# First layer's expert weights loaded with four consecutive rows per partition, context products on every fourth column

## The reference

```
def ec_moe(h, w_router, w_gate, w_up, w_down):
    cap = EC_FACTOR * T // N_EXPERTS
    aff = softmax(h @ w_router)
    gate, idx = top_k(swapaxes(aff, 1, 2), cap)     # each expert picks its tokens
    xe = h[idx]
    hid = silu(xe @ w_gate) * (xe @ w_up)           # per expert, 1024 x 1024 each
    ye = (hid @ w_down) * gate
    return zeros.at[idx].add(ye)
```

## Time and profile before

| | |
|---|---|
| median of three runs | 2534.03 us |
| the profiled execution, its own time | 2537.13 us |
| its span, first to last instruction | 2535.3 us |
| TensorE busy | 2368.9 us (93%) |
| loads by SyncE's and ScalarE's queues | 562.49 MB |

### The profile page before, as it was taken

The page is one execution under the profiler, slowest core; times in us unless marked ns, Lnnn a source line. Parts: engine busy times, 40 slices in busy tenths (PEclk is TensorE's granted clock), DMA queues, the critical chain, the costliest instruction groups (busy, mean ns, idle before and its releaser), DMA issues. The chain is left out here.

```text
span 2535.3 us, 36839 instructions
## 1 busy us (share of the span) xinstructions
PE 2368.9 (93%) x15152; PEld 1506.6 (59%) x15152; DVE 671.8 (26%) x1420; ACT 641.4 (25%) x1154; POOL 571.1 (23%) x320
## 2 busy tenths in 40 slices
PE   5999999999999799999999699999999789999888
PEld 3768878888887344444443477877888633333332
DVE  2271073211033211101111425064112432222223
ACT  4362263221233101111111535244223301100001
POOL 2142321344510001111111224333465000000000
PEclk9999999999998899999999799999999899999999
DMA  6271440221233699999999545343244599999996
GB/s 247 97 287 56 130 115 15 76 73 61 97 136 142 246 387 390 392 388 389 389 387 391 186 163 221 87 104 88 75 133 148 218 362 400 411 413 412 412 411 268
DMA packets 162383, 595.94 MB, mean 235 GB/s; under 512 B 16328, under 2 KB 57680, under 8 KB 143248
## 3 DMA queue, kind: packets, MB, share of 16 engines
q1 hardware_dynamic: 148368, 562.49, 58.7%
q0 software_dynamic: 10432, 25.99, 3.8%
q10 hardware_dynamic: 3488, 6.11, 0.8%
HBM read 576.63 MB, written 21.07 MB: 236 GB/s over the span
## 5 line engine op out<-in xcount | busy, mean ns | idle before, releaser
L473 PE MATMUL ps<-hi_r,ring_r 128*128 128x512 f32 (+1 forms) x1792 | 475.4, 354 | 3.9 <-POOL ring_r L2061 3.9
L1003 PE MATMUL ps<-ring_lo,zone 128*32 128x256 f32 (+1 forms) x3072 | 438.7, 493 | 23.2 <-DMA ring_lo<-in_w_gate 18.9
L473 PEld LDWEIGHTS ps<-hi_r,ring_r 128*128 128x128 f32 x1792 | 317.0, 190 | 51.5 <-POOL ring_r L2061 4.3
L1003 PEld LDWEIGHTS ps<-ring_lo,zone 128*32 128x32 f32 (+1 forms) x3072 | 156.3, 124 | 298.6 <-issue 271.2
L2061 POOL TENSOR_TENSOR ring_r<-ring_lo,ring_r 128x2048 fp32r<-128x2048 f32 (+1 forms) x58 | 240.1, 4144 | 364.9 <-ACT ring_r L1105 332.4
L473 PE MATMUL ps<-lo_r,ring_r 128*128 128x512 f32 (+1 forms) x896 | 315.7, 352 | 0.0
L1013 PE MATMUL ps<-zone 128*64 128x512 f32 (+1 forms) x2048 | 292.5, 496 | 2.3 <-issue 0.3
L467 PE MATMUL ps<-ring_r,hi_r 128*128 128x512 f32 (+1 forms) x736 | 227.7, 392 | 0.9 <-DVE lo_r L1600 0.9
L2170 POOL DMA_INDIRECT zone<-xn_dram,zone x36 | 40.5, 1125 | 812.1 <-DVE zone L2034 744.3
L1013 PEld LDWEIGHTS ps<-zone 128*64 128x64 f32 (+1 forms) x2048 | 111.5, 125 | 166.5 <-issue 146.1
L473 PEld LDWEIGHTS ps<-lo_r,ring_r 128*128 128x128 f32 x896 | 169.9, 190 | 23.3
(11 more groups left out here) (330 smaller groups left out, 2729.7 us busy)
## 6 DMA issues: line engine op xcount, KB each, us to landing
ring_lo<-in_w_gate SPq DMA_DIRECT2D x62, 2048.0 KB, 18.8
zone<-in_w_down SPq DMA_DIRECT2D x62, 2048.0 KB, 19.7
zone<-in_w_up SPq DMA_DIRECT2D x32, 2048.0 KB
ring_lo<-in_w_up SPq DMA_DIRECT2D x30, 2048.0 KB
ring_lo<-in_w_in SPq DMA_DIRECT2D x52, 1024.0 KB, 6.0
ring_lo<-in_ada_w SPq DMA_DIRECT2D x22, 2048.0 KB, 10.9
ring_lo<-in_w_branch SPq DMA_DIRECT2D x24, 512.0 KB, 6.3
zone<-v_dram SPq DMA_DIRECT2D x128, 64.0 KB, 1.9
```

The lines of the kernel that those rows point to most:

```text
L473: i = mm(dst[:, t0:t0 + tw], b[:, kk, f * P:(f + 1) * P], a[:, k, t0:t0 + tw], start=start and n == 0, stop=stop and n == 2)
L1003: i = mm(bank(((2, 4), (3, 5))[s // 2][gi])[j * M:(j + 1) * M, 0:W], xeT[:, k, c0:c0 + M], w[:, k % 4, j * W:(j + 1) * W], start=(k == 0), ...
```

## The change

`near_rows` is now true in both layers. What follows from it in the first layer:

- each unit is loaded with 16 KB runs (line 2302 in place of 2304, and the halves of lines 2291 and 2328 with 8 KB runs);
- the 8 transposes of the tokens and the 4 of the latent hidden values read their stationary operand with a step of four elements (16 bytes);
- GpSimd's queue makes the trip through `mod_dram` in the first layer too, and VectorE scales with `mxA` and `mxS`;
- the context groups of gate and up take columns j, j + 4, j + 8, ... of the weights in place of 256 neighbouring ones, so the moving operand of these products has a step of 16 bytes. Then the hidden value 4n + j stands in group j at column n, and the two context transposes of line 1060 stay contiguous; `out_half` takes `hidC` blocks in the new order.

The waits on `mod_out` count per layer, and the load of `iota` stays in the second layer alone.

```
         def near_rows(l):
-            return l > 0
+            return l >= 0
...
                             i = mm(bank(((2, 4), (3, 5))[s // 2][gi])[j * M:(j + 1) * M, 0:W], xeT[:, k, c0:c0 + M],
-                                   w[:, k % 4, j * W:(j + 1) * W], start=(k == 0), stop=(k == KD - 1))
+                                   w[:, k % 4, j::4] if gi else w[:, k % 4, j * W:(j + 1) * W], start=(k == 0), stop=(k == KD - 1))
...
-                                   hidL[:, k % 4, k // 4, :] if gi == 0 else hidC[:, k % 2, k // 2, :],
+                                   hidL[:, k % 4, k // 4, :] if gi == 0 else hidC[:, k // 4, k % 4, :],
...
                 if near_rows(l):
-                    dve.wait_ge(sem("mod_out"), 64)
+                    dve.wait_ge(sem("mod_out"), 64 * l + 64)
...
-                    pool.wait_ge(sem("mod_out"), 32)
+                    pool.wait_ge(sem("mod_out"), 64 * l + 32)
...
-                if near_rows(l):
+                if l > 0:
                     sp.dma_start(iota, A["iota"]).then_inc(sem("fills_in"), 16)
```

## The result

The changed kernel takes 2660.32 us (median of 4 runs, 2656.15 to 2661.08) against 2533.93 (4 runs, 2533.04 to 2534.76) of the kernel before on the same chip: 1.0492 of it, 95% interval 1.0479 to 1.0505, so 126 us slower. Its profiled execution took 2659.59 us with a span of 2657.7, 122.4 us over the span of before. The forecast was 2541, in a range of 2532 to 2560: the direction was right and the size was not.

The account below looks back on a forecast made before the run. TensorE was taken to bound the first layer's experts, loads the second's. Terms +8.0 + 0.3 + 1.0 - 1.1 - 1.0 = +7.2 us on 2534.0 gave about 2541 us, range 2532 to 2560.

Parts of the forecast that it names:

- What bounds the kernel: First layer's experts bound by TensorE, second layer's by loads; faster first-layer loads worth little, slower TensorE paid 16 times.
- Part 2, the moving operand: Context gate and up products with a step of four: 2 ns more per set over 512 sets, +1.0 us.
- A path that falls to half of its contiguous rate by the step would still give 1.13: Context products: half the merge products' 2.26 columns per ns nearly covers the 1.16 a set streams, supporting almost no cost.
- 33 ns per set: Rival for the context products: stream falls to the strided weight loads' rate, 13 to 33 ns more, 2552 us, chance 0.18.
- The rival of the four streams: Context products' four side-by-side streams get in each other's way: 2653 us two by two, 2880 one by one; chance 0.14.
- Part 1, the transposes: First layer's token and hidden-value transposes with a step of four: +0.50 us per expert, +8.0 us over 16.
- Nothing hides it: The transposes' longer weight load, 141 to 212 ns, is paid in full because TensorE is in order without idle time.
- The first gathered tokens: Their strided transposes ahead of the first layer's expert loop cost about one group's difference, +0.3 us.
- Part 3, the loads: First layer's loads land sooner and their queue stops growing: -1.1 us of waits and -1.0 us after the last expert.
- the last wait: TensorE's remaining waits for weights in the first layer's experts go away, -1.1 us.
- the handover: Chain from scatter to read-back after the first layer's last expert shortens: -1.0 us, bounds 0 and -4.
- Part 4, the trip: First layer's trip through `mod_dram` fits in GpSimd's wait for ScalarE: cost 0, about 17 us if uncovered.

Follow-up runs that it names:

- bench_streams: Kernel before plus fourteen blocks of products, one to four streams, contiguous or stepped, ahead of the expert loop; 256-column sets took 0.2175 us contiguous, 0.454 at step 4.
- stream_only: Kernel before with only the context gate and up products reading columns at a step of four; 2653.9 us, ratio 1.0462.
- no_stride: Changed kernel with the context gate and up products back on 256 neighbouring columns; 2534.41 us, ratio 0.9998.
- pairs: Changed kernel with context groups taking pairs of neighbouring columns, hidden values regrouped and context transposes at a step of two; 2540.88 us, ratio 1.0019.
- bench_types: Kernel before plus blocks of bfloat16 and float32r products and transposes at various steps; bfloat16 at steps 2, 4, 8 took 0.227, 0.451, 0.907 us.
- two_rows: Changed kernel with contiguous context columns, 8 KB runs for first-layer `w_down` and hidden transposes at a step of two; 2533.6 us, ratio 1.0.
- permuted: Changed kernel with the loads of two_rows, ScalarE and VectorE writing values in the order that makes all transposes contiguous; 2531.36 us, ratio 0.9995.

## Why the prediction was right or wrong

**What bounds the kernel** was read rightly, and it gave the direction: TensorE had no slack in the first layer's experts, so faster loads brought 2.5 us and slower products cost their full length.

**Part 2, the moving operand, failed:** taken at +1.0 us, measured at 16 x (41.28 - 33.51 - 0.16) = +122 us, with 33.51 for the pace of before without its waits and 0.16 for the transposes. Per set that is 0.238 us, and the benchmark has 0.454 - 0.2175 = 0.237. `stream_only` has it alone, 16 x 7.62 us, and `no_stride` takes it away. The step that failed is the sentence "A path that falls to half of its contiguous rate by the step would still give 1.13". It set the path's peak by the float32r products of the earlier trace rows and took "half" for the worst. But those products read four columns per line; if a change of line is what is paid, their own 0.227 us for 128 changes is already 1.77 ns each, and 256 changes make 0.454 us, the measured value. Four columns per line against one is a quarter of the rate, not half. (float32r itself does not follow this at a step of four, so that row fits the price but does not explain it.) The neighbour taken as nearest, the strided weight loads of the earlier trace rows, is another reader with another price: 0.118 us for 128 columns, 0.92 ns each, where the moving operand pays 1.77.

The Trainium skill (Advanced Engine Details and Errata, Memory Cachelines) has the rule that decided: at least two hits per 16-byte line, and a penalty for a different line each time. `pairs` and `bench_streams` agree with both halves, 0.226 us at two per line and 0.454 at one. It was cited and then given a price of its own only up to 33 ns per set.

**The rival of the four streams** had 2653 us, nearly the result, for the wrong reason: one stream alone is as slow as four. A time that fits does not show a mechanism.

**Part 1, the transposes, was over-sized:** +8.0 us forecast, 0.16 x 16 = +2.6 measured. The durations were right (1.10 us for the eight, 0.75 for the four, loads of 218 ns). "Nothing hides it" was wrong: the pause ahead of line 1013 fits a wait for ScalarE's copy that the profile doesn't name, and the longer transposes run into it. In the second layer the pause had been read as part of the price. The first gathered tokens cost nothing (1.52 us, before 1.51): TensorE has its lower clock there, where `bench_types` has 0.108 us contiguous and at most 0.120 with the step.

**Part 3, the loads, was right:** the last wait is gone, the landing is a steady 10 us in place of a growing one, and the handover gave 1.0 us, as taken. At TensorE's old pace (`no_stride`) the first layer moves 397 GB/s, the wait stays away and the handover is 1410.15 - 1388.55 = 21.60 us, so the form of the loads is enough for it. In the changed kernel it was not needed: `stream_only`, with the loads of before and the slower TensorE, has no such wait either, a steady landing of 11 us and a handover of 21.53. The number was right, but the changed kernel doesn't show which of the two brought it.

**Part 4, the trip, was right:** no cost, inside GpSimd's wait for ScalarE. TensorE's first gathered tokens come at 843.50 us, before at 842.65, but at 841.94 in `two_rows`, which makes the trip too.

The terms as measured, +122 + 2.6 - 1.5 (waits) - 1.0 = +122.1, make the 122.4 us between the two spans. That the two agree so closely is in part luck: the experts begin 0.85 us later than before, and the rest of the program behind line 514, 1125.2 and 1125.3 us in these two executions, takes 1118.5 to 1121.3 in those of the experiments. The medians are 126 us apart; the profiled execution of before lay 3.1 us above its median.

## What to carry to other kernels

Price a step in the moving operand by lines: count the changes from one 16-byte line to another in a product, at 1.77 ns each (float32 and bfloat16, one stream or four), and pay the larger of that and the contiguous stream; two float32 or four bfloat16 of a line in turn are nearly free. For float32r take 0.85 to 0.91 ns per element in any order that is not contiguous. Take the price of a strided read from a row of the same reader and type, or keep the range open to one element per line, and before a load is made faster at the cost of TensorE's operands, look which of the two has slack.

## What the runs showed of the hardware that was not expected

The count of line changes sets the price for float32 and bfloat16: 1.76 to 1.80 ns per change at steps of 2, 3, 4 and 8, the same for one to four streams, on the same lines or on different ones, at either level of TensorE's clock, and steps of 8 and 16 float32 cost about what a step of 4 does (0.46 and 0.43 us for 256 columns, against 0.454). float32r is the exception: 0.44 ns per element contiguous and 0.85 to 0.91 in the other orders tried, pairs and a step of 8 among them. Order costs the other engines too: ScalarE's 128x1024 write took 2097 ns with neighbouring elements 512 bytes apart (`permuted`), 1138 contiguous.
